# Two weight streams of a mixture-of-experts stage: from one shared queue and a fine weave to two queues and two blocks per chunk

## What is computed

```python
logits = x @ w_router
top_v, top_i = lax.top_k(logits, TOP_K)
gates = jax.nn.softmax(top_v, axis=-1)
combine = jnp.sum(jax.nn.one_hot(top_i, N_EXPERTS) * gates[..., None], axis=1)
out = jnp.zeros_like(x)
for e in range(N_EXPERTS):
    out = out + combine[:, e:e + 1] * _swiglu(x, w_gate[e], w_up[e], w_down[e])

def _swiglu(x, w_gate, w_up, w_down):
    return (jax.nn.silu(x @ w_gate) * (x @ w_up)) @ w_down
```

## Time and profile before

| | us |
|---|---|
| median of 3 runs (1352.99 to 1354.8) | 1353.32 |
| the profiled execution, its own time | 1353.66 |
| its span | 1351.8 |
| PE busy, share of the span | 1322.7, 98% |
| DVE busy | 805.6, 60% |
| ACT busy | 645.7, 48% |
| DMA, mean over the span | 315 GB/s |

### The profile page before, as it was taken

The page is one execution under the profiler, slowest core; times in us unless marked ns, Lnnn a source line. Parts: engine busy times, 40 slices in busy tenths (PEclk is TensorE's granted clock), DMA queues, the critical chain, the costliest instruction groups (busy, mean ns, idle before and its releaser), DMA issues.

```text
span 1351.8 us, 18685 instructions
## 1 busy us (share of the span) xinstructions
PE 1322.7 (98%) x7542; PEld 971.1 (72%) x7542; DVE 805.6 (60%) x971; ACT 645.7 (48%) x687; POOL 4.5 (0%) x12
## 2 busy tenths in 40 slices
PE   9999999999999988999999999999999999999995
PEld 8999999999999866656656655666656565656552
DVE  7555766552988584656565565546665555665523
ACT  7554644342566673544453544444544444444422
POOL 0000000000000000000000000000000000000000
PEclk9999999999999998999999999999999999999998
DMA  8344454453342657999999999999999999999991
GB/s 308 119 150 162 141 181 147 162 213 141 126 182 86 251 224 302 412 427 426 427 392 425 423 423 421 427 384 427 425 417 424 426 391 410 424 426 427 423 424 64
DMA packets 72346, 425.48 MB, mean 315 GB/s; under 512 B 6384, under 2 KB 8432, under 8 KB 27328
## 3 DMA queue, kind: packets, MB, share of 16 engines
q1 hardware_dynamic: 71680, 422.67, 76.9%
q0 software_dynamic: 432, 1.54, 0.3%
q10 hardware_dynamic: 144, 0.02, 0.0%
HBM read 423.16 MB, written 1.05 MB: 314 GB/s over the span
## 4 chain that ended last, share of the span: by engine, by line
PE 86%; DVE 8%; ACT 3%; issue 3%; DMA 0%; DVEq 0%; SPq 0%; ACTq 0%
PE ps L2459 15%; PE ps L2492 8%; PE ps L2392 8%; PE ps L2393 7%; PE ps L2398 7%; PE ps L1842 5%; PE ps L2432 4%; PE ps L1832 4%; PE ps L1833 4%; PE ps L2433 4%; PE ps L2440 4%; PE ps L1880 2%; PE ps L1897 2%; PE ps L1881 2%; DVE wl L1229 1%
## 5 line engine op out<-in xcount | busy, mean ns | idle before, releaser
L1439 DVE TENSOR_TENSOR wl<-raw,wh 128x2048 fp32r<-128x2048 f32 x92 | 210.6, 2291 | 151.2 <-ACT wh L869 151.2
L869 ACT CAST wh<-raw 128x2048 fp32r<-128x2048 f32 x92 | 175.6, 1908 | 174.8 <-issue 101.9
L2392 PE MATMUL ps<-wh,gh 128*128 128x512 f32 x448 | 181.2, 404 | 0.7 <-DVE gl L1512 0.7
L2393 PE MATMUL ps<-wh,gl 128*128 128x512 f32 x448 | 176.9, 395 | 0.0
L2398 PE MATMUL ps<-wl,gh 128*128 128x512 f32 x448 | 120.3, 390 | 0.0
L2459 PE MATMUL ps<-raw,few 128*64 128x512 f32 x256 | 116.7, 598 | 0.0
L2461 PE MATMUL ps<-raw,few 128*64 128x512 f32 x248 | 113.0, 598 | 0.0
L1103 DVE TENSOR_TENSOR wl<-raw,wh 128x4096 fp32r<-128x4096 f32 (+1 forms) x18 | 73.2, 4069 | 61.7 <-ACT wh L628 39.7
L628 ACT CAST wh<-raw 128x4096 fp32r<-128x4096 f32 (+2 forms) x29 | 92.0, 3172 | 34.6 <-PE ps L1833 34.2
L2392 PEld LDWEIGHTS ps<-wh,gh 128*128 128x128 f32 x448 | 85.3, 190 | 27.7 <-issue 9.7
L1439 DVE TENSOR_TENSOR wl<-unsplit,wh 128x2048 fp32r<-128x2048 f32 x29 | 66.4, 2291 | 55.8 <-ACT wh L869 55.8
(11 more groups left out here) (357 smaller groups left out, 2631.9 us busy)
## 6 DMA issues: line engine op xcount, KB each, us to landing
raw<-in_moe_w_up SPq DMA_DIRECT2D x65, 1024.0 KB, 11.5
raw<-in_moe_w_gate SPq DMA_DIRECT2D x62, 1024.0 KB, 10.6
raw<-in_moe_w_down SPq DMA_DIRECT2D x59, 1024.0 KB, 10.2
unsplit<-in_moe_w_down SPq DMA_DIRECT2D x23, 1024.0 KB, 9.9
unsplit<-in_moe_w_up SPq DMA_DIRECT2D x20, 1024.0 KB, 11.1
unsplit<-in_moe_w_gate SPq DMA_DIRECT2D x17, 1024.0 KB, 10.4
raw<-in_diff_w_qkv SPq DMA_DIRECT2D x8, 1536.0 KB, 6.4
sq<-in_moe_w_gate SPq DMA_DIRECT2D x12, 1024.0 KB, 10.3
```

Of the source, the lines that this page charges most:

```text
L869: act.copy(split_piece(wh, p), landing("wide", p)).then_inc(wh_ready, 1)
L1439: dve.tensor_tensor(split_piece(wl, p), landing("wide", p), raw_f(split_piece(wh, p)), ALU.subtract).then_inc(wl_ready, 1)
L2392: pe.matmul(ps[:, bank, :], bm["gh"][:, s], w, start=(k0 + k == 0), stop=False)
L2393: ins = pe.matmul(ps[:, bank, :], bm["gl"][:, s], w, start=False, stop=False)
```

## The change

**Two queues and two rings.** Buffers 0 to 5 become the wide ring, 6 to 10 the few ring. At the start all eleven hold wide pieces 0 to 10; then wide piece p waits for the wide piece six places earlier in its ring, and few piece p for the few piece five places earlier. SP issues the wide pieces alone; POOL issues the few ones (`load_few`), after `routed`.

**Two blocks per chunk.** PE now does all wide work of a step (gate, up, scatters, down, wide turn) and then all few work (few turn, two halves of few up, two of few down, with the gather parts between them). ACT and DVE follow the same order. `few_turn` writes to PSUM bank 0 instead of 4, so the next wide gate waits for its copy. `wide_turn(0)`, `gather_few`, `count_units` and `list_units` move about one step later.

The sixth piece of a chunk (the second down half) goes into the buffer of the chunk's first (`raw_more`). The diff, cut to its core:

```diff
-LAG, AHEAD = 2, 3
+LAG = 2
 WITH_FEW = P + SMALL
 PARTS = KD // 2
+FEW_TURNS = 0
+LAST_SUMS = (2, 3, 5, FEW_TURNS)
...
+        few_landed = {i: sem(f"few_landed{i}") for i in ROUND[6:]}
...
-        def piece_order():
-
-            order, few_from = [], []
-            for s in range(CHUNKS + LAG + 1):
-                t = s - LAG
-                wide = [wide_at[kind, s] + half for kind in "gu" for half in range(2)] if s < CHUNKS else [None] * 4
-                few = [few_up_at(t) + half for half in range(4)] if 0 <= t < CHUNKS else [None] * 4
-                wide += [wide_at["d", s - 1] + half for half in range(2)] if 1 <= s <= CHUNKS else [None] * 2
-                few += [few_down_at(t - 1) + half for half in range(2)] if 1 <= t <= CHUNKS else [None] * 2
-                for a, b in ((0, 2), (2, 4), (4, 5), (5, 6)):
-                    order += [("wide", p) for p in wide[a:b] if p is not None]
-                    order += [("few", p) for p in few[a:b] if p is not None]
-            sooner = sorted(range(len(order)), key=lambda n: n - AHEAD * (order[n][0] == "wide"))
-            return [order[n] for n in sooner]
-
-        pieces = piece_order()
-        position = {piece: q for q, piece in enumerate(pieces)}
+        wide_ring, few_ring = ROUND[:6], ROUND[6:]
+        held_in = [[("wide", s)] for s in ROUND]
+        for p in range(RAW_SLOTS, STREAM):
+            held_in[wide_ring[(p - RAW_SLOTS) % len(wide_ring)]].append(("wide", p))
+        for p in range(STREAM):
+            held_in[few_ring[p % len(few_ring)]].append(("few", p))
+        position = {piece: (s, n) for s, held in enumerate(held_in) for n, piece in enumerate(held)}
...
-            q = position[kind, p]
-            return piece_landed[q % RAW_SLOTS], 16 * (q // RAW_SLOTS + 1)
+            s, n = position[kind, p]
+            return (piece_landed[s], 16 * (n + 1)) if kind == "wide" else (few_landed[s], 16 * n)
...
-                    held, of = pieces[q - RAW_SLOTS]
-                    if held == "wide":
-                        sp.wait_ge(wl_ready, C_MOE + of + 1)
-                    else:
-                        sp.wait_ge(few_used, of + 1)
-                if stream == "wide":
-                    (kind, i), half = wide_chunks[p // 2], p % 2
-                else:
-                    kind, i, half = few_pieces[p]
-                unit = (stream, i // FC)
-                if unit not in numbers_of:
-                    if unit == ("few", 0):
-                        sp.wait_ge(routed, 1)
-                    numbers_of[unit] = expert(2 * unit[1] + (stream == "few"))
-                load_piece(numbers_of[unit], raw_place(s), s, kind, i % FC, half)
+                    sp.wait_ge(wl_ready, C_MOE + held_in[s][n - 1][1] + 1)
...
+            def load_few(e, s, kind, i, half):
+
+                source = weights_of[kind][bass.ds(e * (FC * 2 * P) + P * (2 * i + half), P), :]
+                pool.dma_start(raw_place(s), source).then_inc(few_landed[s], 16)
+
+            pool.wait_ge(routed, 1)
+            for p, (kind, i, half) in enumerate(few_pieces):
+                s, n = position["few", p]
+                held, of = held_in[s][n - 1]
+                if held == "wide":
+                    pool.wait_ge(wl_ready, C_MOE + of + 1)
+                else:
+                    pool.wait_ge(few_used, of + 1)
+                if kind == "g" and i % FC == 0 and half == 0:
+                    u = 2 * (i // FC) + 1
+                    before_e, e = e if i else None, pool.value_load(bm["unit_i"][0:1, u:u + 1], min_val=0, max_val=E - 1)
+                last_of_unit = kind == "d" and i % FC == FC - 1 and i + 1 < CHUNKS
+                load_few(before_e if last_of_unit else e, s, kind, i % FC, half)
...
+                    if s == 1:
+                        turned_high(0)
...
+            def turned_few(c):
+
+                dve.wait_ge(few_turned, c + 1)
+                turned = ps[:, FEW_TURNS, :].rearrange("p (k s) -> p k s", s=P)[:, :, SMALL:]
+                dve.tensor_copy(bm["few_act"][:, c % 2, :].rearrange("p (k s) -> p k s", s=SMALL), turned).then_inc(few_act_ready, 1)
...
-                    if s == 0:
+                    if s == 1:
...
+                if kind == "g" and c > LAG + 1:
+                    pe.wait_ge(few_act_ready, c - LAG - 1)
...
-                pe.wait_ge(eal_ready, min(c + LAG + 1, CHUNKS))
+                pe.wait_ge(esil_ready, min(c + LAG + 2, CHUNKS))
                 for k in range(4):
                     s = slice(k * P, (k + 1) * P)
-                    ins = pe.transpose(ps[:, 4, s], few_prod_[:, s], ident)
+                    ins = pe.transpose(ps[:, FEW_TURNS, s], few_prod_[:, s], ident)
...
                 if s < CHUNKS:
                     wide_up(s, "g")
-                if 0 <= t < CHUNKS:
-                    few_up(t, 0)
-                if 1 <= t < CHUNKS:
-                    few_turn(t - 1)
+                    if s == 1:
+                        wide_turn(0)
                 if adds and r == 2:
                     scatter_wide(n - 1, 2)
                 if adds and r == 4:
@@ -2511,21 +2516,7 @@
                     wide_up(s, "u")
                 if s == CHUNKS + 1:
                     scatter_wide(WIDE_UNITS - 1, 0)
-                    scatter_wide(WIDE_UNITS - 1, 1, 0)
-                if 0 <= t < CHUNKS:
-                    few_up(t, 1)
-                if gathers:
-                    gather_part(n + 1, 0)
-                if 1 <= s <= CHUNKS:
-                    wide_down(s - 1, 0)
-                if s < CHUNKS:
-                    wide_turn(s)
-                if gathers:
-                    gather_part(n + 1, 1)
-                if 1 <= t <= CHUNKS:
-                    few_down(t - 1, 0)
-                if t == CHUNKS - 1:
-                    few_turn(t)
+                    scatter_wide(WIDE_UNITS - 1, 1, 1)
                 if adds and r == 1:
                     scatter_wide(n - 1, 0)
                 if adds and r == 2:
@@ -2535,26 +2526,42 @@
                 if adds and r == 4:
                     scatter_few(n - 1, 3)
                 if 1 <= s <= CHUNKS:
+                    wide_down(s - 1, 0)
                     wide_down(s - 1, 1)
-                if gathers:
-                    gather_part(n + 1, 2)
-                if 1 <= t <= CHUNKS:
-                    few_down(t - 1, 1)
                 if adds and r == 1:
                     scatter_wide(n - 1, 1)
                 if adds and r == 3:
                     scatter_few(n - 1, 1)
+                if 1 <= s < CHUNKS:
+                    wide_turn(s)
+                if s == LAG:
+                    gather_few()
+                if 1 <= t < CHUNKS:
+                    few_turn(t - 1)
+                if 0 <= t < CHUNKS:
+                    if gathers:
+                        gather_part(n + 1, 0)
+                    few_up(t, 0)
+                    if gathers:
+                        gather_part(n + 1, 1)
+                    few_up(t, 1)
+                if gathers:
+                    gather_part(n + 1, 2)
+                if 1 <= t <= CHUNKS:
+                    few_down(t - 1, 0)
+                if t == CHUNKS - 1:
+                    few_turn(t)
                 if gathers:
                     gather_part(n + 1, 3)
-                if s == 1:
-                    gather_few()
+                if 1 <= t <= CHUNKS:
+                    few_down(t - 1, 1)
                 if s < CHUNKS and r == 4:
                     turn_picks(n)
                 if s == CHUNKS + 1:
-                    scatter_wide(WIDE_UNITS - 1, 2, 1)
+                    scatter_wide(WIDE_UNITS - 1, 2, 4)
                     scatter_wide(WIDE_UNITS - 1, 3)
             for k in range(2 * QT):
-                scatter_few(FEW - 1, k, 2 + k)
+                scatter_few(FEW - 1, k, LAST_SUMS[k])
```

More of the change, by code:

```diff
@@ L454, in more_in @@
             times = sum(1 for at_ in MORE_PLACES if at_[0] == s)
-            so_far = sum(1 for q in range(len(pieces)) if q % RAW_SLOTS == s)
+            so_far = sum(1 for kind, of in held_in[s] if kind == "wide")
             return piece_landed[s], 16 * (times * a + so_far - times * WIDE_UNITS + sum(1 for at_ in MORE_PLACES[:p + 1] if at_[0] == s))
@@ L531, in load_piece @@
                 sp.dma_start(to, source).then_inc(piece_landed[s], 16)
[L533 to L545 removed]
+            for p in range(STREAM):
+                (kind, i), half = wide_chunks[p // 2], p % 2
+                s, n = position["wide", p]
+                if p < 6:
+                    sp.wait_ge(wl_ready, max(c for c in range(C_MOE) if c % 3 == min(p // 2, 2)) + 1)
+                elif p < 9:
+                    sp.wait_ge(wl_ready if p == 6 else w_used, C_MOE)
+                elif p == 9:
@@ L569, in load_more @@
+                last_of_unit = kind == "d" and i % FC == FC - 1 and i + 1 < CHUNKS
+                load_piece(before_e if last_of_unit else e, raw_place(s), s, kind, i % FC, half)
```

(4 more changed lines are left out.)

147 lines of the change are left out of this document (66 added, 81 removed).

## The result

The changed kernel takes **1426.16 us** (median of 4 runs, 1422.42 to 1430.03) against 1353.15 us (1352.66 to 1354.8) for the kernel before on the same chip: ratio 1.0533, 95% interval 1.052 to 1.0545. It is slower by 73 us, where 1357.7 was forecast and 1392 was the upper end of the range. The profiled execution of the kernel after took 1426.89 us with a span of 1425.2.

The account below looks back on a forecast made before the run. PE was taken as the bound, with the DMA 2% behind. The sum was 1353.7 - 24 + 3 + 33 - 10 + 2 = 1357.7 us, with a range of 1326 to 1392.

Parts of the forecast that it names:

- The bound: Experts' stage: PE never waits for a piece and is the bound, with the DMA 2% behind.
- Part 1: Chunks without a gather: fewer changes between wide and few work on PE save 1.1 us each, -24 us.
- Part 2: Three chunks with a gather: gather part 2 waits for bank 7 to be cleared, +3 us (0 to +6).
- Part 3: Second few-down half: PE waits 1.5 us a chunk without a gather for the sixth few piece, +33 us.
- the landing: Sixth few piece from issue to landing: 4.9 us on an idle DMA, 6.4 to 6.6 with a wide piece sharing.
- The piece beside: Wide piece SP issues some 0.9 us behind the buffer's release: shares the DMA engines, 1.5 us more landing time.
- Part 4: Kernel start: PE's waits of 3.8 and 4.5 us and the slow clock behind them go, -10 us (-4 to -13).
- Part 5: Steps 28 to 30, only few pieces left: PE waits once or twice for 1 us, +2 us (0 to +5).
- the piece in time: Rival at the second few-down half: sixth few piece lands with 0.3 us of wait, 1331 us; chance 0.29.
- The second: Rival: POOL's piece waits for the SP piece in progress, a wait of 3 us a chunk, 1391 us; chance 0.17.
- DVE's hold on GpSimd's descriptors: Rival at the buffer's release: DVE's split holds up POOL's descriptors, +15, 1373 us; chance 0.06.
- Late splits: Rival in the wide block: PE waits for splits, 1 us a chunk more, 1383 us; chance 0.06.

Follow-up runs that it names:

- five_six: The changed kernel with its eleven buffers dealt five to the wide ring and six to the few ring: 1335.31 us, ratio 0.9858 to the kernel before.
- hold: The changed kernel, SyncE holding back the wide piece due 4 us ahead of the sixth few piece until that sixth has landed: 1370.03 us.
- start: The kernel before with only the change's moves at the start, its order, ring and queue kept: 1349.17 us, ratio 0.9958.
- two_queues: The kernel before with only the change's loading (two rings, two queues), its order of work kept: 1354.76 us, ratio 1.0001.

## Why the prediction was wrong, step by step

**The bound.** Right: PE, with the DMA 2% behind. five_six showed both, a plain chunk shorter on PE and then the DMA at 427 GB/s.

**Part 1, fewer changes: right.** Forecast 1.1 us a chunk; 29.5 - 28.4 = 1.1 measured in the plain chunks of five_six, and the few block runs without an edge.

**Part 2, the gather chunks: the wait was right, its follow-up missing.** A wait of 2.1 was forecast, 1.9 measured, 5.7 in all. What was missing: such a chunk gains nothing from fewer changes. It takes 36.1 in the kernel after against 34.2, the whole wait more, where the forecast took 1.1 off for it. In five_six the clock also falls behind the wait, another 1.7 us, so such a chunk takes 3.6 more than before instead of 1.0.

**Part 3, the sixth piece: right place, wrong size.** This is the step that failed, and a term for the clock was missing beside it.

First **the landing**: forecast 6.4 to 6.6 us, measured 8.1 on average. The notice itself was 4.8 instead of 5.0, so the mean wait was 3.3 instead of 1.5, 69.8 us instead of 33. Two things were wrong in it.

The piece beside was to start 0.9 us behind the release and to share, for 1.5 more. It was issued only 0.4 us behind the release, and in 20 of 21 chunks GpSimd's piece did not send a packet for 2.2 to 3.9 us, while SP's was moving. Where SP's piece passes whole before the sixth has landed, the prediction's own 2.45 us for 1 MB apply: 4.9 + 2.45 = 7.4, and 9 chunks show 7.3 to 7.5.

And wide pieces still in progress were put at nothing ("here one at most, just ending"), yet in hold, with the two nearest pieces held back, 1.3 us of wait a chunk stay, and 7 chunks of the kernel after take 9.0 to 10.0. How the missing 1.8 us of wait divide between the two is not settled: in the net of the runs the piece beside cost just the 1.5 reckoned, and the ones in progress the rest.

Second, **the clock**. The text reckons with a slow clock at the start and nowhere else, though the earlier trace rows shows 0.54 behind waits of 4 us. Regular waits of 3 us bring it too: 64.8 us at the lower level, 29 to 32 lost. No term of the sum had it.

These pieces make up the 25 chunks: 22 x -1.1 = -24, +69.8 for the sixth piece, +5.7 for the gathers' waits and 29 to 32 for the clock are 80 to 84, and 83.0 was measured.

**Part 4, the start: the size was near, the reason half right.** -10 was forecast, -14.2 measured. Both waits of the earlier trace rows are gone, and the 3 us of new ones that the forecast took back came to 1.3. But start on its own brings 5.6, and five_six reaches its fourth chunk at 545.18. That the kernel after gets there at 537.20 would fit its few ring, which takes five pieces rather than six ahead of time, so that part of the gain is work of the DMA put off, or its wide ring of six buffers rather than five; no run shows either alone.

**Part 5, the end:** +2 forecast, +4.5 measured.

**The rivals.** The first, the piece in time, gives 1331 and is what five_six reaches (1335), with another deal of buffers. "Against it: the DMA would then be saturated" was wrong: with a chunk's notice a saturated DMA does no harm. The second was nearest: it had the late start of GpSimd's piece behind SP's and the right wait (3 against 3.3), and gives 1391; with the clock's 32 us it would have been 1423. The late start is shown, by the first packet after 1.2 us alone and 2.2 to 3.9 with a piece of SP's beside it; why the packets wait is not. The rival was given 0.17 and carried the range's upper end, to which the clock was not added. DVE's hold on GpSimd's descriptors: hold speaks against it. In the chunk shown DVE has the same work at the issue in both kernels, a split that ends 0.1 us behind it and two subtractions, yet the first packet comes after 1.2 us in hold and 2.9 in the kernel after. Late splits: PE waits 0.6 us for them in all, so no.

## What to carry to other kernels

A ring's worth is the time between a buffer's release and its next use, read on the consuming engine for each position of the ring, and not the number of buffers: an order that bundles the uses of one ring shortens just that time. Give the ring one buffer for each piece of a bundle before anything else; here that turned +5.3% into -1.4%. And price every regular wait of PE twice, once for its length and once for the clock behind it.

## What the runs showed of the hardware

- Waits of about 3 us, one per 33 us, are enough for the granted clock to fall to 0.5 (1.2 GHz) for 3.4 or 6.8 us behind many of them: 15 stretches in 25 chunks. With 3.2 us of extra matmuls in the wait, 3 were left. In five_six it fell behind waits of 1.9 us.
- A DMA that has run out of work takes some 2 us from the issues to its full rate (133 GB/s over 2.10 us with a piece on each queue). For 1 MB alone it is 5.0 to 5.1 us from issue to landing on GpSimd's queue and 5.0 on SyncE's.
- Two 1 MB pieces issued 0.1 us apart on two queues both slow down and land after 6.2 (SyncE's) and 7.5 us (GpSimd's), where one alone takes 5.0. GpSimd's loses the more although it was issued first: its first packet came 2.9 us behind its issue there, and 1.2 us behind it in hold, without SyncE's.
- The software's queue reached the DMA's full rate: two_queues carries 419 GB/s over 24 chunks, as before, with half of the pieces on GpSimd.
